# Sigmoid and silu gates written as exponential, logarithm and exponential, with a product on GpSimd

## The chip, the cores and the metric

One core of a Trainium2 chip runs the whole program. The metric is the device time of one execution in microseconds (us). The kernel before took 3142.65 us, the median of 3 runs (3142.52 to 3145.22).

## What is computed

The program is a stack of blocks on 512 tokens of width 1024 in float32. Only its first part matters here: two layers (L = 0, 1) that mix three branches. A convolution branch, a neighbourhood attention over a grid (branch br = 0, 8 heads) and a window attention (br = 1, 8 heads) read one projection of the input. Each is gated, projected, gated again and summed. Layer 0 also carries 256 context tokens, so its tiles have 768 columns; those of layer 1 have 512.

```python
def merge_branches(a_glu, a_gate, o_na, n_gate, o_wa, w_gate, merge, ...):
    y_a = conv_branch(a_glu, a_gate, ...)
    y_b = (o_na * jax.nn.silu(n_gate)) @ w_proj_b
    y_c = (o_wa * jax.nn.silu(w_gate)) @ w_proj_c
    g_a, g_b, g_c = jnp.split(merge, 3, axis=-1)
    y = jax.nn.sigmoid(g_a) * y_a + jax.nn.sigmoid(g_b) * y_b + jax.nn.sigmoid(g_c) * y_c
    return y @ w_o
```

Each of the four silu gates of a layer and branch (units `ag`, 128 channels, two heads each) multiplies the attention's output. The sigmoid gates (`mg` for the attention branches, `cm` for the convolution's; eight of each per layer and branch) multiply the projected outputs.

## The kernel before

TensorE does every product with each float32 operand split in a high and a low part, in three matmuls: 8 steps of 3 matmuls per 512 columns make one chunk of 128 output channels ("lin" steps, line 1795). ScalarE rounds each weight tile (`WH<-RAW`, line 1106) and VectorE takes the rest (`WL<-RAW,WH`, line 1116); for some chunks of the window attention of layer 1 GpSimd does both (lines 1134 and 1125).

`branch` writes the order of the mixing out by hand as a list of units; every engine walks through the same list and takes from it what is its own, so a unit's place in the list is its place in each engine's queue. Attention runs in five phases, one per pair of heads. The scores, exponentials and values of pair p are laid between the projection steps of the chunks for pair p + 1 (`woven`), and a chunk's own after-work is put a number of steps behind its start by `chain`: 8 is right behind its last step. On ScalarE the exponentials of the scores (`Pa<-PS`, `Pb<-PS`, line 1997), the row of maxima (`QB<-PS`, line 2056), the logarithm and exponential of the softmax's denominator (`O<-PS`, `O<-O`, lines 2079 and 2082), the copies of queries and keys (line 2048) and the weight roundings stand in one queue with the gates.

A gate in the woven part is the unit `gev` (silu) or `mgev` (sigmoid) at step 8: one activation from PSUM into one of six tiles T (line 1981). The function tables of silu and of sigmoid are not the one that has exponential and logarithm, so a table load goes before the activation, and behind it the program loads `natural_log_exp_and_others` again (line 1983):

```python
act.activation(buf((nm, "g"))[:, 0:ntk], pairs.of(nm)[:, 0:ntk], ACT.Silu if u[0] == "gev" else ACT.Sigmoid)
if nm not in tail:
    act.preload_act_table_set("natural_log_exp_and_others")
```

The unit `gate`, behind each phase, multiplies the attention's output by the silu gate on GpSimd (`O<-O,T`, line 2286). GpSimd's queue also has copies of queries and keys (line 2270) and the DMAs of the bias tables (BS, line 2291, and BT, line 2296). VectorE lays the taps of the convolution (`C<-AP,SMA,C`, line 1636) between its other work, in the neighbourhood branch alone. The PSUM tiles of the projections are a ring (`pairs`), of which attention borrows two; a gate's PSUM tile is free when its last reader is done. Gates of the tail behind the attention (unit lists `merge` and `proj`) follow one another without a change of table back. `pe_keep` puts a few matmuls of constants in front of certain units (line 1772).

Of the kernel before, what the change touches and what calls it, by code (L numbers as in the profile page):

```python
# [10 lines left out]
ALU = mybir.AluOpType  # L11
# [254 lines left out]
class Plan:  # L266
# [125 lines left out]
    def branch(self, L, br):  # L392
# [11 lines left out]
        def chain(kind, m):  # L404
            nm = (kind, L, br, m)
            if kind == "av":
                return {8: [("vev", nm)], 10: [("vt", nm)], 12: [("vout", nm)]} if br else {8: [("vev", nm)]}
            if kind == "ag":
                return {8: [("gev", nm)]}
            if kind == "mg":  # L410
                return {8: [("mgev", nm)]}
            if kind == "cm":
                return {8: [("mgev", (kind, L, 0, m))], 12: [("paev", ("pa", L, 0, m))]}
            c = {8: [("nrm1", nm)], 11: [("nrm2", nm)], 13 if br else 14: [("nrm3", nm)]}
            if L and br and kind == "aq" and m:
                return {8: [("nrm1", nm)], 12: [("nrm2", nm)], 14: [("nrm3", nm)], 18: [("rot", nm)], 20: [("rot2", nm)]}
            if br:
                c[15] = [("rot", nm)]
                c[16] = [("rot2", nm)]
            return c  # L420
# [68 lines left out]
        for ph in range(5):  # L489
# [26 lines left out]
                    at.setdefault(1 if f else 22 if L and br else 18, []).extend(to)  # L516
            made, late = woven(steps, at, 0, n, heads(ph - 1))
            order += tapped(made, 3 if L == 0 else 5, ph > 0) + ([("gate", L, br, ph - 1, f) for f in range(2)] if ph else [])
        assert not late
        if L == 0 and br:  # L520
            order[4:4] = [("modend", L, 2)]
        order += [("split", ("ag", L, br, m)) for m in range(4)]
# [45 lines left out]
    def attn(self, L, br):  # L568
# [9 lines left out]
        for u in order:  # L578
# [33 lines left out]
            elif kind in ("gev", "mgev"):  # L612
                tmp.take((nm, "g"))
                pairs.release(nm, (nm, "g"))
            elif kind == "pjev":
                pairs.release(nm, ("yp",) + nm[1:] if br else ("y", L, 0, nm[3]))
                tmp.release((("mg",) + nm[1:], "g"), ("y", L, 2 * br, nm[3]))
# [305 lines left out]
def build(nc, t, out):  # L923
# [5 lines left out]
    with ctx:  # L929
# [1011 lines left out]
        def act_attn(act, L, br):  # L1941
            ntk = NTK[L]
# [4 lines left out]
            for u in P.orders[L, br]:  # L1947
# [23 lines left out]
                elif u[0] == "out":  # L1971
                    act_out(act, L, br, nm, u[2])
                elif u[0] == "vev":
                    for dst, src in moved(br, "av", buf((nm, "v")), pairs.of(nm), NT):
                        for w in due("act", ("lin", nm), was((nm, "v"))):
                            act.wait_ge(*w)
                        act.activation(dst, src, ACT.Copy).then_inc(*did("act_v", (nm, "v")))
                elif u[0] in ("gev", "mgev"):
                    for w in due("act", ("lin", nm), was((nm, "g"))):
                        act.wait_ge(*w)  # L1980
                    act.activation(buf((nm, "g"))[:, 0:ntk], pairs.of(nm)[:, 0:ntk], ACT.Silu if u[0] == "gev" else ACT.Sigmoid).then_inc(*did("act_gate", (nm, "g")))  # L1981
                    if nm not in tail:
                        act.preload_act_table_set("natural_log_exp_and_others")
                elif u[0] == "tr":
                    act_rows(act, L, br, u, B)
                elif u[0] == "es":
                    act_sink(act, L, br, u)
                elif u[0] == "fin":
                    act_fin(act, L, br, u)
                elif u[0] == "st":  # L1990
                    p, f, k = u[3:]
                    n = sum(x[2] for x in score_parts(L, br)[k])
                    biased = not br and 2 <= k < 4
                    R = P.pts[L, br]
                    for w in due("act", ("ba" if biased else "sc",) + u[1:], R.after[u], ("masks", L) if br else ("attn", L, br)):
                        act.wait_ge(*w)
                    act.activation(PT[L, br][R.of(u)][:, 0:n], B.of(u)[:, 0:n], ACT.Exp).then_inc(*did("act_ex", ("ex",) + u[1:]))
                elif u[0] == "split":
                    m = nm[3]
                    if m == 0:  # L2000
                        here("act", ("attnout", L, br))
                    for dst, src in gated(L, br, AGH[L, br][:, m, :], OO[L, br][:, m, :]):
                        for w in due("act", ("gated", L, br, m, 0), ("gated", L, br, m, 1), ("attnout", L, br)):
                            act.wait_ge(*w)
                        act.activation(dst, src, ACT.Copy).then_inc(*did("act_g", (nm, "hi")))
# [235 lines left out]
        def pool_attn(pool, L, br):  # L2241
# [11 lines left out]
            for u in P.orders[L, br]:  # L2253
# [4 lines left out]
                elif u[0] == "out" and not (L and br):  # L2258
# [7 lines left out]
                    for dst, at, key in to:  # L2266
                        for w in due("pool", (nm, "y2") if br else (nm, "y"), scores_read(L, br, p - 1, f), ("turn", done["turn"])):
                            pool.wait_ge(*w)
                        done["turn"] += 1
                        pool.tensor_copy(dst, y[at:at + 64, 0:n]).then_inc(*did("pool_st", (nm, key), (nm, "out", f), ("turn", done["turn"])))  # L2270
                elif u[0] == "max" and not br and u[5] == 3 and (u[3], u[4]) != (3, 1):
                    pool_bias_by_query(pool, L, 2 * u[3] + u[4] + 1, [("mx", L, br, u[3], u[4], j) for j in range(4)])
                elif u[0] == "st" and not br and u[5] == 3 and (u[3], u[4]) != (3, 1):
# [1215 lines left out]
```

## Time and profile before

| | us |
|---|---|
| median of 3 runs | 3142.65 |
| the profiled execution, its own time | 3145.4 |
| its span | 3143.6 |
| TensorE matmuls busy | 3029.9 |
| VectorE busy | 1858.6 |
| ScalarE busy | 1282.9 |
| GpSimd busy | 263.7 |
| ScalarE table loads, lines 1981 and 1983 | 50.0 and 41.1 |

The profiled execution took 1.8 us more than its span, and 2.75 us more than the median. Times in the trace are counted from the span's start. The attention phases lie at 190 to 400 us (layer 0, neighbourhood), 650 to 906 (layer 0, window), 1110 to 1340 (layer 1, neighbourhood) and 1440 to 1680 (layer 1, window). Busy shares are averages over stages with different limits; an engine's waits are listed with what released it.

### The profile page before, as it was taken

How to read it: one execution, taken by the hardware profiler on the slowest of the kernel's cores; microseconds unless marked ns; L12 is line 12 of the kernel's file. 1: busy time of each engine (PE TensorE's matmuls, PEld its weight loads, DVE VectorE, ACT ScalarE, POOL GpSimd, SP SyncE). 2: the span in 40 equal slices, each digit the busy share in tenths (PEclk: the TensorE clock that was granted, in tenths of full speed). 3: DMA queues.
4: the chain of work that ended last, by engine and by line, in shares of the span. 5: the costliest groups of instructions: out<-in, count | busy, mean ns of one | idle time of the engine just before them, and what ended most of it. 6: DMA issues, size and time to landing. Idle time of an engine off the chain costs nothing.

```text
span 3143.6 us, 36963 instructions
## 1 busy us (share of the span) xinstructions
PE 3029.9 (96%) x14782; PEld 2393.2 (76%) x14782; DVE 1858.6 (59%) x2959; ACT 1282.9 (41%) x1989; POOL 263.7 (8%) x206
## 2 busy tenths in 40 slices
PE   8999999999999998999999999999999989999998
PEld 5878877877788676767777777788888866788887
DVE  5877675255435667685443787666435675566632
ACT  3244523135532344534554475322225656422222
POOL 0011100001100001102110031000003210000000
PEclk9999999999999999999999999999999989999999
DMA  5222132320012322222112233232332310233332
GB/s 207 72 69 74 48 101 96 109 86 28 21 34 78 104 81 81 67 81 69 47 54 67 83 99 93 94 94 94 96 96 88 121 38 1 81 94 94 94 94 74
DMA packets 78731, 251.49 MB, mean 80 GB/s; under 512 B 9121, under 2 KB 11169, under 8 KB 78561
## 3 DMA queue, kind: packets, MB, share of 16 engines
q1 hardware_dynamic: 72672, 227.91, 22.9%
q0 software_dynamic: 5024, 18.09, 1.8%
q8 instruction: 117, 1.92, 0.3%
q10 hardware_dynamic: 864, 3.15, 0.3%
q14 instruction: 54, 0.43, 0.0%
HBM read 247.01 MB, written 2.10 MB: 79 GB/s over the span
## 4 chain that ended last, share of the span: by engine, by line
PE 45%; ACT 4%; DVE 3%; issue 1%; DMA 0%; POOL 0%; DVEq 0%; ACTq 0%
PE PS L1157 31%; PE PS L1795 4%; PE PS L2815 3%; PE PS L2910 1%; PE PS L1919 1%; ACT WH L1106 1%; PE PS L2875 0%; PE PS L2891 0%; PE PS L2837 0%; ACT PS L2958 0%; PE PS L2876 0%; PE PS L2892 0%; ACT PTN L2972 0%; ACT L1981 0%; PE PS L2543 0%
## 5 line engine op out<-in xcount | busy, mean ns | idle before, releaser
L1116 DVE TENSOR_TENSOR WL<-RAW,WH 128x1024 fp32r<-128x1024 f32 (+3 forms) x374 | 423.7, 1134 | 527.5 <-ACT WH L1106 526.9
L1106 ACT ACTIVATE WH<-RAW 128x1024 fp32r<-128x1024 f32 (+3 forms) x397 | 384.6, 972 | 435.3 <-PE PS L1157 331.0
L1795 PE MATMUL PS<-Hh,WH 128*128 128x512 f32 x1376 | 525.0, 382 | 14.5 <-DVE WL L1116 7.9
L1795 PE MATMUL PS<-Hl,WH 128*128 128x512 f32 x1376 | 487.4, 354 | 0.0
L1795 PE MATMUL PS<-Hh,WL 128*128 128x512 f32 x1376 | 486.1, 353 | 0.0
L1795 PEld LDWEIGHTS PS<-Hh,WH 128*128 128x128 f32 x1376 | 260.0, 189 | 74.6 <-issue 22.7
L1157 PE MATMUL PS<-XH,WH 128*128 128x512 f32 x768 | 305.1, 397 | 0.0
L1157 PE MATMUL PS<-XH,WL 128*128 128x512 f32 x768 | 303.5, 395 | 0.0
L1157 PE MATMUL PS<-XL,WH 128*128 128x512 f32 x768 | 303.5, 395 | 0.0
L1795 PEld LDWEIGHTS PS<-Hl,WH 128*128 128x128 f32 x1376 | 260.3, 189 | 47.6 <-issue 10.1
L1795 PEld LDWEIGHTS PS<-Hh,WL 128*128 128x128 f32 x1376 | 260.3, 189 | 40.3
L1636 DVE SCALAR_TENSOR_TENSOR C<-AP,SMA,C 128x512 f32<-128x512 f32 x360 | 227.0, 692 | 0.5
L1157 PEld LDWEIGHTS PS<-XL,WH 128*128 128x128 f32 x768 | 144.0, 188 | 36.0 <-issue 1.0
L1157 PEld LDWEIGHTS PS<-XH,WH 128*128 128x128 f32 x768 | 144.0, 188 | 35.9 <-issue 1.0
L1157 PEld LDWEIGHTS PS<-XH,WL 128*128 128x128 f32 x768 | 144.0, 187 | 35.2
L1157 PE MATMUL PS<-FGh,WH 128*128 128x512 f32 x384 | 152.2, 396 | 0.0
L1157 PE MATMUL PS<-FGh,WL 128*128 128x512 f32 x384 | 151.8, 395 | 0.0
L1157 PE MATMUL PS<-FGl,WH 128*128 128x512 f32 x384 | 151.7, 395 | 0.0
L1157 PE MATMUL PS<-Hh,WH 128*128 128x512 f32 (+1 forms) x384 | 138.8, 362 | 2.0 <-DVE Hl L1243 1.9
L1157 PE MATMUL PS<-Hl,WH 128*128 128x512 f32 (+1 forms) x384 | 137.1, 357 | 0.0
L1157 PE MATMUL PS<-Hh,WL 128*128 128x512 f32 (+1 forms) x384 | 137.1, 357 | 0.0
L2472 ACT ACTIVATE U<-U 128x512 f32<-128x512 f32 x48 | 30.4, 633 | 253.1 <-DVE U L2503 253.1
(401 smaller groups left out, 5742.1 us busy)
## 6 DMA issues: line engine op xcount, KB each, us to landing
RAW<-in_w_in SPq DMA_DIRECT2D x124, 512.0 KB, 3.6
RAW<-in_ffn_in SPq DMA_DIRECT2D x96, 512.0 KB, 3.6
RAW<-in_ffn_out SPq DMA_DIRECT2D x48, 512.0 KB, 3.5
RAW<-in_w_ada SPq DMA_DIRECT2D x32, 384.0 KB, 3.7
RAW<-in_nsa_in SPq DMA_DIRECT2D x21, 512.0 KB, 3.3
RAW<-in_lru_in SPq DMA_DIRECT2D x20, 512.0 KB, 3.6
MW<-in_w_ada SPq DMA_DIRECT2D x32, 256.0 KB, 9.7
BS<-in_bs POOLq DMA_DIRECT2D x16, 512.0 KB, 3.9
```

Source lines behind the costliest of these rows:

```text
L1106: act.activation(WH[half[j]][:, 0:n], RAW[j % NRAW][:, 0:n], ACT.Copy).then_inc(*did("act_whi", ("whi", j)))
L1116: dve.tensor_tensor(WL[half[j]][:, 0:n], RAW[j % NRAW][:, 0:n], WH[half[j]][:, 0:n].bitcast(F32), ALU.subtract).then_inc(*did("dve_wlo", ( ...
L1157: mm = pe.matmul(ps[:, c:c + n], wt[:, 128 * i:128 * i + 128], x[:, a:a + n], start=(seen == 0 and q == 0), stop=(seen == total - 1 and q ...
L1636: dve.scalar_tensor_tensor(dst, src, wt, dst, ALU.mult, ALU.add).then_inc(*did("dve_tap", ("tap", L, m, k, a0), ("tap", L, m, k)))
L1795: mm = pe.matmul(ps[:, c:c + w_], wt[:, 128 * k:128 * k + 128], x[:, a:a + w_], start=(k == 0 and q == 0), stop=(k == n - 1 and q == 2))
L1919: mm = pe.matmul(dst, VV[L, br][:, b, 64 * g:64 * g + 128], src, start=first, stop=end)
L2472: act.activation(u, u, ACT.Gelu_apprx_tanh).then_inc(*did("act_ge", (a, "gelu")))
L2815: mm = pe.matmul(ps[:, 0:S], wt[half[j]][:, 128 * k:128 * k + 128], x[:, k, :], start=(k == 0 and q == 0), stop=(k == 7 and q == 2))
L2910: mm = pe.matmul(o[64 * f:64 * f + 64, 0:256].rearrange("p (m q) -> p m q", m=2), VN[b][:, kt, g, :], pt[:, f, :, :], start=(b == 0 and kt ...
```

## The change

The woven gates become chains of small steps that need the exponential and logarithm alone: sigmoid(x) = exp(-ln(1 + exp(-x))). `gx1` and `sx1` take exp(-x) from PSUM; `gx1` also copies x out of PSUM into a second tile. `gx2` is ln(1 + e), `gx3` the last exponential. `gx4` multiplies by x on GpSimd, for silu alone. The gates of the tail stay as they were. What is left of the after-work when the last phase ends is now appended to the list, ahead of `split`; before, nothing was.

```diff
             if kind == "ag":
-                return {8: [("gev", nm)]}
+                return {8: [("gx1", nm)], 10: [("gx2", nm)], 11: [("gx3", nm)], 12: [("gx4", nm)]}
             if kind == "mg":
-                return {8: [("mgev", nm)]}
+                return {8: [("sx1", nm)], 10: [("gx2", nm)], 11: [("gx3", nm)]}
             if kind == "cm":
-                return {8: [("mgev", (kind, L, 0, m))], 12: [("paev", ("pa", L, 0, m))]}
+                nm = (kind, L, 0, m)
+                return {8: [("sx1", nm)], 9: [("gx2", nm)], 10: [("gx3", nm)], 12: [("paev", ("pa", L, 0, m))]}
...
-        assert not late
+        for k in sorted(late):
+            order += late[k]
...
+            elif kind == "gx1":
+                tmp.take((nm, "x"))
+                tmp.take((nm, "g"))
+                pairs.release(nm, (nm, "x"), (nm, "e"))
+            elif kind == "sx1":
+                tmp.take((nm, "g"))
+                pairs.release(nm, (nm, "e"))
+            elif kind == "gx4":
+                tmp.release((nm, "x"), (nm, "g"))
...
+                elif u[0] in ("gx1", "sx1"):
+                    if u[0] == "gx1":
+                        for w in due("act", ("lin", nm), was((nm, "x"))):
+                            act.wait_ge(*w)
+                        act.activation(buf((nm, "x"))[:, 0:ntk], pairs.of(nm)[:, 0:ntk], ACT.Copy).then_inc(*did("act_gate", (nm, "x")))
+                    for w in due("act", ("lin", nm), was((nm, "g"))):
+                        act.wait_ge(*w)
+                    act.activation(buf((nm, "g"))[:, 0:ntk], pairs.of(nm)[:, 0:ntk], ACT.Exp, scale=-1.0).then_inc(*did("act_gate", (nm, "e")))
+                elif u[0] == "gx2":
...
+                    act.activation(g, g, ACT.Ln, bias=ones[:, 0:1]).then_inc(*did("act_gate", (nm, "l")))
+                elif u[0] == "gx3":
...
+                    act.activation(g, g, ACT.Exp, scale=-1.0).then_inc(*did("act_gate", (nm, "s" if nm[0] == "ag" else "g")))
...
+                elif u[0] == "gx4":
+                    g = buf((nm, "g"))[:, 0:ntk]
+                    for w in due("pool", (nm, "s"), (nm, "x"), ("turn", done["turn"])):
+                        pool.wait_ge(*w)
+                    done["turn"] += 1
+                    pool.tensor_tensor(g, g, buf((nm, "x"))[:, 0:ntk], ALU.mult).then_inc(*did("pool_g", (nm, "g"), ("turn", done["turn"])))
```

It touches 33 gates: 16 silu (8 per layer) and 17 sigmoid (7 in layer 0, 10 in layer 1). Counted over ScalarE's whole program, 67 of 109 table loads go and 82 activations come; GpSimd gets 16 products. The queues of TensorE, VectorE and SyncE keep their rows and their order.

ScalarE in the window attention of layer 1, at a sigmoid gate (`cm`); in the rows `T<-PS` is the gate, QB the row of maxima and WH a weight rounding. Before:

```order
739 L2079 ACTIVATE O<-PS 64x512
740 L2082 ACTIVATE O<-O 64x512
741 L2048 ACTIVATE QA<-T 64x512
742 L2048 ACTIVATE QB<-T 64x512
743 L1981 ACT_TABLE_LOAD
744 L1981 ACTIVATE T<-PS 128x512
745 L1983 ACT_TABLE_LOAD
746 L2056 ACTIVATE QB<-PS 1x512
747 L1106 ACTIVATE WH<-RAW 128x512
748 L1997 ACTIVATE Pb<-PS 128x512
```

Now (the lines of the changed file are 11 to 35 further down):

```order
754 L2077 ACTIVATE QA<-T 64x512
755 L2077 ACTIVATE QB<-T 64x512
756 L1996 ACTIVATE T<-PS 128x512
757 L2085 ACTIVATE QB<-PS 1x512
758 L1117 ACTIVATE WH<-RAW 128x512
759 L2001 ACTIVATE T<-T,CO 128x512
760 L2006 ACTIVATE T<-T 128x512
761 L2026 ACTIVATE Pb<-PS 128x512
```

Both loads are gone: only the gate's one activation is left between the copies and the row of maxima. The logarithm and the last exponential come behind the weight rounding.

ScalarE in the neighbourhood attention of layer 0, at the second silu gate. Before:

```order
116 L2056 ACTIVATE QB<-PS 1x512
117 L1981 ACT_TABLE_LOAD
118 L1981 ACTIVATE T<-PS 128x768
119 L1983 ACT_TABLE_LOAD
120 L2056 ACTIVATE QB<-PS 1x256
121 L1106 ACTIVATE WH<-RAW 128x1024
122 L2048 ACTIVATE KA<-T 64x768 x2
123 L2048 ACTIVATE QA<-T 64x768
124 L1997 ACTIVATE Pb<-PS 128x512
125 L1997 ACTIVATE Pa<-PS 128x512
```

Now:

```order
118 L1993 ACTIVATE T<-PS 128x768
119 L1996 ACTIVATE T<-PS 128x768
120 L2085 ACTIVATE QB<-PS 1x256
121 L1117 ACTIVATE WH<-RAW 128x1024
122 L2001 ACTIVATE T<-T,CO 128x768
123 L2077 ACTIVATE KA<-T 64x768 x2
124 L2077 ACTIVATE QA<-T 64x768
125 L2026 ACTIVATE Pb<-PS 128x512
126 L2006 ACTIVATE T<-T 128x768
127 L2026 ACTIVATE Pa<-PS 128x512
```

Two activations from PSUM stand for the one with its loads, one more is ahead of the exponentials of the scores, and one between them.

GpSimd at the same place (T is the gate, BT and BS the bias tables). Before:

```order
29 L2270 CAST QB<-T 64x768
30 L2296 DMA BT<-in_bt 128x1024
31 L2291 DMA BS<-in_bs 128x1024
32 L2286 TENSOR_TENSOR O<-O,T 64x512
33 L2286 TENSOR_TENSOR O<-O,T 64x256
```

Now:

```order
30 L2299 CAST QB<-T 64x768
31 L2305 TENSOR_TENSOR T<-T 128x768
32 L2331 DMA BT<-in_bt 128x1024
33 L2326 DMA BS<-in_bs 128x1024
34 L2321 TENSOR_TENSOR O<-O,T 64x512
```

The new product stands between a copy and the issue of the next bias table.

## Rows read from the trace of the kernel before

**Rows 1.** The page: span, and busy time of each engine.
```profile
span 3143.6 us, 36963 instructions
PE 3029.9 (96%) x14782; PEld 2393.2 (76%) x14782; DVE 1858.6 (59%) x2959; ACT 1282.9 (41%) x1989; POOL 263.7 (8%) x206
```

**Rows 2.** Busy time by stretch: PE, PEld, DVE, ACT, POOL, then PEclk, DMA share, GB/s.
```profile
190.00:400.00 210.00, 200.51 (x1102) 167.00 (x1103) 150.66 (x235) 107.87 (x155) 38.04 (x38) 1.00 0.20 63
650.00:906.00 256.00, 243.47 (x1302) 197.05 (x1301) 120.26 (x175) 124.60 (x181) 23.36 (x17) 1.00 0.09 29
1110.00:1340.00 230.00, 210.33 (x1019) 163.51 (x1017) 158.10 (x269) 113.10 (x174) 32.59 (x34) 1.00 0.23 71
1440.00:1680.00 240.00, 226.94 (x1037) 173.49 (x1036) 112.34 (x176) 123.01 (x181) 39.84 (x24) 0.99 0.16 50
```

**Rows 3.** TensorE's waits, 190 to 1700 us: us in total, times, longest.
```profile
PE PS L1899 <- ACT QB L2056: 5.9, 6, 1.8
...
PE PS L1866 <- DVE STAT L2212: 5.8, 5, 2.1
PE PS L1919 <- ACT Pa L1997: 5.5, 7, 1.3
...
PE PS L1919 <- ACT Pb L1997: 4.6, 6, 1.0
...
PE PS L1899 <- ACT Pa L1997: 2.1, 2, 1.2
...
PE PS L1795 <- DVE Gl L2139: 1.4, 2, 0.7
...
PE PS L1841 <- ACT T L1981: 1.2, 2, 0.6
```

**Rows 4.** ScalarE's groups by shape, 190 to 1700 us: busy us, mean ns.
```profile
L1981 ACT ACT_TABLE_LOAD x39 | 50.0, 1283 | 11.3 <-PE PS L1795 10.8
L1983 ACT ACT_TABLE_LOAD x32 | 41.1, 1283 | 0.6
...
L1981 ACT ACTIVATE T<-PS 128x768 f32<-128x768 f32 x32 | 26.0, 812 | 108.2 <-PE PS L1795 108.0
```

**Rows 5.** ScalarE in order of time at one sigmoid gate: start us, us.
```profile
1506.92 1.28 ACT L1981 ACT_TABLE_LOAD   x1 [0.56 <-PE PS L1795]
1508.22 0.60 ACT L1981 ACTIVATE T<-PS 128x512 f32<-128x512 f32 x1
1508.83 1.28 ACT L1983 ACT_TABLE_LOAD   x1
1510.13 0.58 ACT L2056 ACTIVATE QB<-PS 1x512 fp32r<-1x512 f32 x1
```

**Rows 6.** TensorE in order of time, at three of its waits.
```profile
262.35 1.12 PE L1919 MATMUL PS<-Pb,V 128*128 128x512 f32 x2 [0.72 <-ACT Pb L1997]
...
1510.76 0.50 PE L1899 MATMUL PS<-QA,KA 128*128 128x512 f32 x1 [1.41 <-ACT QB L2056]
...
1655.97 0.59 PE L1899 MATMUL PS<-QA,KA 128*128 128x512 f32 x1 [1.76 <-ACT QB L2056]
```

**Rows 7.** Busy time by stretch, around the third of them.
```profile
1656.00:1659.00 3.00, 3.00 (x8) 2.33 (x9) 0.56 (x1) 1.70 (x3) 0.00 (x0) 0.54 0.29 87
```

**Rows 8.** VectorE and GpSimd in order of time, layer 0, neighbourhood.
```profile
263.59 1.15 DVE L1636 SCALAR_TENSOR_TENSOR C<-AP,SMA,C 128x512 f32<-128x512 f32 x2
...
265.05 0.70 DVE L2129 TENSOR_TENSOR PS<-PS,BT 128x512 f32<-128x512 f32 x1 [0.31 <-PE PS L1900]
...
338.19 3.37 DVE L1636 SCALAR_TENSOR_TENSOR C<-AP,SMA,C 128x512 f32<-128x512 f32 x2
...
338.56 2.71 POOL L2286 TENSOR_TENSOR O<-O,T 64x512 f32<-64x512 f32 x2
```

**Rows 9.** GpSimd products: mean ns by shape, and one alone in time.
```profile
L2286 POOL TENSOR_TENSOR O<-O,T 64x768 f32<-64x768 f32 x8 | 14.6, 1830 | 98.8 <-DVE O L2239 93.1 <-ACT T L1981 5.5 <-POOL QB L2270 0.2
...
1653.16 1.28 POOL L2286 TENSOR_TENSOR O<-O,T 64x512 f32<-64x512 f32 x1 [19.49 <-DVE O L2239]
```

More of the change, by code:

```diff
@@ L1977, in act_attn @@
                         act.activation(dst, src, ACT.Copy).then_inc(*did("act_v", (nm, "v")))
+                elif u[0] in ("gx1", "sx1"):
[8 more added lines that the diff above has]
+                    g = buf((nm, "g"))[:, 0:ntk]
+                    for w in due("act", (nm, "e"), ("co",)):
+                        act.wait_ge(*w)
+                    act.activation(g, g, ACT.Ln, bias=ones[:, 0:1]).then_inc(*did("act_gate", (nm, "l")))
+                elif u[0] == "gx3":
+                    g = buf((nm, "g"))[:, 0:ntk]
+                    for w in due("act", (nm, "l")):
+                        act.wait_ge(*w)
+                    act.activation(g, g, ACT.Exp, scale=-1.0).then_inc(*did("act_gate", (nm, "s" if nm[0] == "ag" else "g")))
                 elif u[0] in ("gev", "mgev"):
@@ L2270, in pool_attn @@
                         pool.tensor_copy(dst, y[at:at + 64, 0:n]).then_inc(*did("pool_st", (nm, key), (nm, "out", f), ("turn", done["turn"])))
+                elif u[0] == "gx4":
+                    g = buf((nm, "g"))[:, 0:ntk]
+                    for w in due("pool", (nm, "s"), (nm, "x"), ("turn", done["turn"])):
+                        pool.wait_ge(*w)
+                    done["turn"] += 1
+                    pool.tensor_tensor(g, g, buf((nm, "x"))[:, 0:ntk], ALU.mult).then_inc(*did("pool_g", (nm, "g"), ("turn", done["turn"])))
                 elif u[0] == "max" and not br and u[5] == 3 and (u[3], u[4]) != (3, 1):
```

## The prediction

> **What bounds the kernel now.** The page first: TensorE's matmuls are busy for 3029.9 of 3143.6 us, ScalarE for 1282.9 [rows 1]. So TensorE is the bound, and a change on ScalarE can only give back what TensorE waits for it. Its own instructions don't change: its queue keeps every row. Next the four attention stretches, where all touched gates lie [rows 2]: 936 us, of which TensorE is busy for 881.3. The 54.8 us left are all that any change of waits could give there. Third, who ended those waits [rows 3]. The five ScalarE rows make 19.3 us (one more, for a PSUM tile that a gate held, has 0.6). The rest is for VectorE, mainly norm and maximum chains that begin with TensorE's own results, so they move with it.
>
> Fourth, what a gate costs ScalarE's queue. A load takes 1.28 us, an activation of 768 columns 0.81 [rows 4], one of 512 columns 0.60 [rows 5]. The instructions behind a load start within 0.02 us of its end: at 1506.92 the load, at 1508.22 the gate, at 1508.83 the load back, at 1510.13 the row of maxima that TensorE has been waiting for, 1.41 us [rows 5, 6]. A gate thus holds the queue for 3.37 us in layer 0 (1.28 + 0.81 + 1.28) and 3.16 in layer 1, and the loads are three quarters of it.
>
> **ScalarE, by place in its queue.** Busy time: 67 loads go, 67 x 1.283 = 86.0 us. 82 activations come: in layer 0 three for each of 8 silus and two for each of 7 sigmoids, 38 at 0.81; in layer 1 8 x 3 + 10 x 2 = 44 at 0.60; together 57.2 us. Net 28.8 us less, to about 1254. What counts is how early the next instruction starts. In layer 0, behind a silu gate's first step (copy and exponential), the queue is 3.37 - 1.62 = 1.75 us ahead of before; behind the logarithm 0.94; behind the last exponential 0.13. Behind a sigmoid gate 2.56, 1.75 and 0.94. In layer 1 the silu gives 1.96, 1.36 and 0.76, the sigmoid 2.56, 1.96 and 1.36. None is negative: by work queued, nothing on ScalarE comes later than before. A PSUM tile is free sooner too: 1.62 us after a silu gate begins where it was 2.09.
>
> The trace in order of time has 22 waits of TensorE for ScalarE, of 0.3 to 1.8 us, within 8 us of a gate's second load: 8 in layer 0 (6.2 us), 5 in layer 1's neighbourhood attention (3.4), 9 in its window attention (8.5); three of them stand in rows 6. I took each against the lead at its place in the new order. The wait of 0.72 us at 262.35 [rows 6] is for Pb, behind the logarithm of a silu: the lead of 0.94 takes it away. The 1.41 at 1510.76 has a lead of 2.56. The 1.76 at 1655.97 is for a row of maxima behind a weight rounding and a logarithm, lead 1.36: 0.4 stays. Of the pair 0.89 and 0.80 around 1635 to 1638, 1.36 of 1.69 goes; one of 0.35 in layer 0 keeps 0.22. Sum: 6.0 + 3.4 + 7.7 = **17.1 us**.
>
> Two chains through ScalarE end on VectorE. One wait of 1.28 us for a maximum, one of the five in rows 3, is for a VectorE queue that had stood still for a weight rounding behind a gate: 1.2 us. The two for Gl at the attention's ends, 1.4 us [rows 3], follow from softmax denominators that stood behind a load: 1.3 us. The late logarithms and exponentials of the last gates, which now stand ahead of the split, lie beside VectorE's and GpSimd's work on the same heads; uncovered they would cost 2 x 0.81. That makes 19.6 us.
>
> **GpSimd and VectorE.** 16 products come: 8 of 768 columns at 1.83 us and 8 of 512 at 1.28 [rows 9], 24.9 us, if the time goes by columns. GpSimd is busy for 263.7 us [rows 1], but its new product can hold others. A pair of convolution taps takes 1.15 us alone and 3.37 beside a GpSimd product; that product, a 512 and a 256 part, took 2.71 too [rows 8]. So the two engines don't run two-operand work from SBUF side by side. The neighbourhood attention has taps and VectorE busy for 69 to 72% of the time; the window attention has no taps and 47% [rows 2]. The first layer 0 products come some 0.3 us after the first of these taps at 263.59. The bias addition at 265.05 [rows 8] is right behind them, and an exponential and TensorE's next values hang on it. A product in front can push it by up to 1.8 us. Bounds: nothing, if each product falls into an idle stretch or if the two share without loss; 24.9 us, if all 16 stand in TensorE's way in full. The row nearest is that of the taps, which only the 8 neighbourhood products meet: I take 0.4 us each, **3 us**, well towards the lower end, since TensorE's waits for maxima at present, 5 in 190 to 1700 us, are 5.8 us in all though GpSimd's two-operand parts already run there (24 in the two neighbourhood stretches). The bias table's DMA issue now stands behind the product. GpSimd is busy for only 38.0 of 210 us there [rows 2], so that idle queue covers it; without that cover it would be 1.83 us late.
>
> The Trainium skill has this as a rule ("SBUF — State Buffer", summary for kernel authors): a VectorE operation with two SBUF inputs and a GpSimd one that reads SBUF exclude each other, the second waits for the first to finish. The taps agree with it. By that rule each meeting costs the length of the other operation, which is the upper end above.
>
> **What the lead is worth.** A wait taken away makes TensorE come sooner to the next one. Chains that start from its own results follow; those that are paced by VectorE's queue do not, above all in layer 1's neighbourhood attention (VectorE 69%, TensorE idle for 19.7 of 230 us [rows 2]). Bounds: nothing lost, or half of 19.6. I take 3 us.
>
> Sum: 19.6 - 3 - 3 = **13.6 us**. The profiled execution's 3145.4 us becomes 3131.8. The median of the runs is 2.75 below the profiled execution; from 3142.65 the forecast is **3129.0 us**.
>
> On the table loads the skill speaks otherwise than the rows. "ScalarE: Activation LUTs" (section on what a table load costs) puts a switch at about 2.66 us, a load of 1.28 and a drain of 1.38. Rows 5 show no drain: gate and load follow within 0.02 us. By the page 67 switches would be 178 us of ScalarE's time, an estimate; the waits of TensorE are measured and their sum would hardly change.
>
> **Rivals.**
>
> *All of it, and the clock.* TensorE's clock is at the upper of its two levels (2.4 GHz, granted 1.00) nearly throughout; after the wait of 1.76 us it was granted 0.54 for 3 us [rows 7], mostly the lower level, 1.2 GHz. Such a spell costs 3 x 0.46 = 1.4 us. If the wait is cut to 0.4 and the spell goes with it, and neither VectorE's queue nor the products take anything, the gain is 19.6 + 1.4 = 21.0 us: 3121.6. For it: the leads are two to four times as long as most waits. Against it: VectorE's load in the neighbourhood stretches. 0.17.
>
> *The waits move instead.* The row of maxima or the exponential that TensorE waited for arrives sooner, but its next need then waits for VectorE, and the last exponential of the gate stands in front of a score's exponential where the lead is only 0.13. Price: half the gain of the window stretches (4.4 us in layer 0 and 7.7 in layer 1) and none of the neighbourhood's, less 3 for the products: 3.0 us, 3139.6, which is within 0.2%. For it: 35 of the 54.8 us of idle time aren't ScalarE's. 0.17.
>
> *The products stop VectorE where TensorE waits for it.* Slower by this one mechanism: each product makes taps, weight remainders (`WL`) or the copies' remainders wait for its full length, and the PSUM bank of a maximum comes free that much later. All 16 in full are 24.9 us against 19.6: slower by 5.3, 3148. With the excess of the taps in rows 8 (3.37 - 1.15 = 2.2 us for a product's two parts) 16 meetings would be 35 us and 3158. It decides from 1.2 us of exposed waiting per product. Against it: only half of the products meet taps, and in the window stretches VectorE is idle for half of the time. 0.05.
>
> *The change doesn't do what it says.* A load could stay where a step needs another table. The new order has no load between the woven steps, so this has 0.01, with the time of before.
>
> **Numbers.** Forecast 0.60, from 3124 to 3136. A measurement of this kernel can tell about 0.2%, 6.3 us: faster means below 3136.4. Faster: 0.60 and 0.17, and 0.03 of the moved waits, 0.80. Within 0.2%: the rest of the moved waits and some of the products, 0.16. Slower: 0.04. The range goes from 3121 to 3140: it takes in the whole gain and most of the moved waits, and leaves out the slower case.
>
> **What would show it.** 42 table loads on ScalarE in all, and its busy time near 1254 us; GpSimd near 289; TensorE's busy time within 3 us of before. TensorE's waits for QB, Pa and Pb from 18.1 us (the first four ScalarE rows of rows 3) to under 4; the ones at 1510.76 and 262.35 gone, that at 1655.97 at 0.4 or less. Waits for the maxima (L2212) would grow by up to 3 us. It is wrong if the waits for ScalarE go and the time doesn't follow; if they stay, though the loads are gone; or if taps beside the new products make the bias additions late by more than 1 us each.

## The result, and the profile after

The changed kernel took 3119.1 us, the median of 5 runs (3116.5 to 3122.3), against 3143.75 for the kernel before in the same comparison (5 runs, 3142.5 to 3149.5). The ratio is 0.9919, with a 95% interval of 0.9905 to 0.9932: 24.6 us faster. The forecast was 13.6 us, and the result lies 2 us below the lower end of the range. A second comparison, on another chip (with the experiments, below), gave 3121.2 against 3144.1, ratio 0.9924 [0.9911, 0.9936], 22.9 us; its median would lie just inside that end.

The page of the changed kernel, span and busy time of each engine, against [rows 1]:

```profile
span 3120.5 us, 37010 instructions
PE 3027.4 (97%) x14782; PEld 2395.6 (77%) x14782; DVE 1868.7 (60%) x2959; ACT 1252.7 (40%) x2004; POOL 304.7 (10%) x222
```

ScalarE is at 1252.7 us where 1254 were forecast, and TensorE's busy time is 2.5 us less. GpSimd has 41.0 us more, where 24.9 had been counted for the products. The stretches between (names of columns as in [rows 2]) say where the time went:

```profile
190.00:400.00 210.00, 201.37 (x1111) 168.36 (x1111) 157.80 (x238) 106.04 (x162) 54.18 (x42) 1.00 0.21 63
650.00:906.00 256.00, 249.16 (x1341) 203.13 (x1341) 126.77 (x181) 125.43 (x190) 30.76 (x21) 1.00 0.10 31
1110.00:1340.00 230.00, 213.49 (x1029) 166.90 (x1028) 166.44 (x272) 108.97 (x181) 42.88 (x38) 0.99 0.23 73
1440.00:1680.00 240.00, 235.35 (x1075) 182.08 (x1074) 116.45 (x177) 111.23 (x187) 40.31 (x24) 0.99 0.16 50
```

These are stretches of time and hold somewhat later work than before. In both window stretches TensorE is idle for much less, 6.8 and 4.7 us for 12.5 and 13.1. In the first neighbourhood stretch it is idle for 8.6 us, and was for 9.5: there little came. That can be read to the microsecond, since TensorE's queue has the same matmuls in the same order: set beside each other by their number, the changed kernel is 0.2 us behind at 645 us, 6.9 ahead at 906, 12.2 at 1340 and 22.4 at 1680. The stretch from 1735 to the end adds 0.7: a low-clock spell there was longer before.

TensorE's waits, 190 to 1700 us of the changed kernel, against [rows 3]:

```profile
PE PS L1806 <- DVE WL L1127: 9.9, 9, 2.9
PE PS L1859 <- ACT T L2049: 5.9, 5, 1.9
...
PE PS L1877 <- DVE STAT L2241: 4.5, 4, 2.1
...
PE PS L1930 <- ACT Pb L2026: 3.5, 3, 1.4
...
PE PS L1910 <- ACT Pa L2026: 0.9, 1, 0.9
PE PS L1930 <- ACT Pa L2026: 0.8, 1, 0.8
...
PE PS L1910 <- ACT Pb L2026: 0.4, 1, 0.4
```

No wait for QB is left (5.9 us before) and none for a gate's PSUM tile. Waits for Pa and Pb fell from 12.2 to 5.6 us, of which 2.5 are new (below), and those for maxima from 5.8 to 4.5. What stays on top is behind VectorE's weight remainders (10.1 us before) and behind T L2049, the inverse roots of the queries' and keys' norms (5.9 before too): the gates hardly touch these.

ScalarE's groups by shape, same stretch, against [rows 4]:

```profile
L2001 ACT ACTIVATE T<-T,CO 128x768 f32<-128x768 f32 x15 | 14.0, 930 | 0.2
...
L2001 ACT ACTIVATE T<-T,CO 128x512 f32<-128x512 f32 x18 | 12.9, 715 | 0.1
L2006 ACT ACTIVATE T<-T 128x768 f32<-128x768 f32 x15 | 12.6, 839 | 0.2
```

The logarithm takes 0.93 us for 768 columns and 0.72 for 512, 0.12 more than the 0.81 and 0.60 of the prediction, and the last exponential 0.84. So the smallest lead of the prediction, 0.13 us behind a silu gate of layer 0, was in truth none (3.37 - 1.62 - 0.93 - 0.84 = -0.02).

Now one place, the sigmoid gate of [rows 5]. TensorE in order of time before, the matmul ahead of the wait and the second one behind it (between them stands the one of 1510.76, [rows 6]):

```profile
1508.96 0.40 PE L1795 MATMUL PS<-CGh,WL 128*128 128x512 f32 x1
...
1511.10 0.39 PE L1900 MATMUL PS<-QB,KB 65*128 65x512 f32 x1
```

The same three in the changed kernel:

```profile
1496.48 0.39 PE L1806 MATMUL PS<-CGh,WL 128*128 128x512 f32 x1
1496.71 0.40 PE L1910 MATMUL PS<-QA,KA 128*128 128x512 f32 x1
1496.94 0.39 PE L1911 MATMUL PS<-QB,KB 65*128 65x512 f32 x1
```

The idle time shown was 1.41 us. From start to start it was 1.80 before and is 0.23 now, 1.57 less; then 0.34 before and 0.23 now, 0.11 less. Together the gate gave back 1.68 us, 0.27 more than the idle time. The difference has two parts that the rows show: a matmul of 0.40 us lies over its successor's start by 0.17 when nothing waits, and the first one behind a wait starts its successor 0.11 late. (The profile models the ends of matmuls, so idle time between them is a modelled figure; the starts are not.)

A gate can also cost TensorE time where the view shows no idle time at all. Before, at a silu gate of layer 0:

```profile
257.99 0.27 PE L1795 MATMUL PS<-Hh,WL 128*128 128x256 f32 x1
258.31 0.50 PE L1899 MATMUL PS<-QA,KA 128*128 128x512 f32 x1
```

and in the changed kernel:

```profile
258.04 0.28 PE L1806 MATMUL PS<-Hh,WL 128*128 128x256 f32 x1
258.16 0.40 PE L1910 MATMUL PS<-QA,KA 128*128 128x512 f32 x1
```

From start to start 0.32 us became 0.12. The view lists no wait, since the matmul before it covers all but 0.04 us.

Last, ScalarE's order in the changed kernel at the sigmoid gate above:

```profile
1494.37 0.60 ACT L1996 ACTIVATE T<-PS 128x512 f32<-128x512 f32 x1 [0.49 <-PE PS L1806]
1494.99 0.59 ACT L2085 ACTIVATE QB<-PS 1x512 fp32r<-1x512 f32 x1
1495.61 0.63 ACT L1117 ACTIVATE WH<-RAW 128x512 fp32r<-128x512 f32 x1
```

The row of maxima is done at 1495.58, 1.1 us before TensorE comes for it.

### The profile page after: what moved, and what is told of

Read it like the earlier page. It is cut to its first block, busy times and chain, and to the rows that moved or that the text cites. A ratio compares the mean times of both kernels' runs of the same rounds, so it can differ in the third digit from the quotient of the medians.

```text
span 3120.5 us, 37010 instructions
## 1 busy us (share of the span) xinstructions
PE 3027.4 (97%) x14782; PEld 2395.6 (77%) x14782; DVE 1868.7 (60%) x2959; ACT 1252.7 (40%) x2004; POOL 304.7 (10%) x222
## 3 DMA queue, kind: packets, MB, share of 16 engines
q1 hardware_dynamic: 72672, 227.91, 22.9%
## 4 chain that ended last, share of the span: by engine, by line
PE 47%; ACT 3%; DVE 3%; issue 1%; DMA 0%; DVEq 0%; ACTq 0%
PE PS L1168 32%; PE PS L1806 5%; PE PS L2850 3%; PE PS L2945 1%; PE PS L1930 1%; PE PS L2910 0%; ACT WH L1117 0%; PE PS L2926 0%; PE PS L2872 0%; ACT PS L2993 0%; PE PS L2911 0%; PE PS L2927 0%; ACT PTN L3007 0%; PE PS L2578 0%; PE PS L1910 0%
## 5 line engine op out<-in xcount | busy, mean ns | idle before, releaser
L1806 PEld LDWEIGHTS PS<-Hh,WH 128*128 128x128 f32 x1376 | 260.5, 189 | 74.3 <-issue 21.6
L1806 PEld LDWEIGHTS PS<-Hl,WH 128*128 128x128 f32 x1376 | 260.9, 190 | 48.3 <-issue 10.1
L1136 POOL TENSOR_TENSOR WL<-RAW,WH 128x1024 fp32r<-128x1024 f32 (+1 forms) x33 | 78.8, 2389 | 572.3 <-ACT WH L1117 571.5
```

Of the source, the lines that this page charges most:

```text
L1136: pool.tensor_tensor(WL[half[j]][:, 0:n], RAW[j % NRAW][:, 0:n], WH[half[j]][:, 0:n].bitcast(F32), ALU.subtract).then_inc(*did("pool_wlo", ...
L1806: mm = pe.matmul(ps[:, c:c + w_], wt[:, 128 * k:128 * k + 128], x[:, a:a + w_], start=(k == 0 and q == 0), stop=(k == n - 1 and q == 2))
```

## The experiments

**An account of the time.** The traces are compared on one stretch that is cut by matmuls, not by time: from TensorE's matmul that started at 190.17 before to the one at 1735.17. It holds all four attention stretches. In it I take three sums: the idle time shown for TensorE's waits (those of over 0.15 us, which the view lists), their number, and the time in which the granted clock was 0.5, that is at the lower of the two levels, 1.2 GHz. Such a spell is charged with half of its length. The theory that the first comparison gave: *gain = waits less, by the idle time shown, + 0.27 us for each wait fewer, + half of the low-clock time less.* The 0.27 comes from places of the first trace pair; the other kernels test it.

| kernel | waits, us (number) | low clock, us | gain by the account | gain measured |
|---|---|---|---|---|
| before | 71.4 (78) | 10.2 | | |
| changed | 52.3 (52) | 17.1 | 22.7 | 22.6 |
| changed, again | 51.8 (52) | 10.2 | 26.6 | 26.2 |
| exponential alone | 49.4 (51) | 20.5 | 24.2 | 25.2 |
| no product | 50.6 (50) | 13.7 | 26.6 | 26.3 |
| product on VectorE | 51.7 (52) | 20.5 | 21.6 | 21.6 |
| window gates only | 57.6 (62) | 17.1 | 14.7 | 14.1 |
| neighbourhood gates only | 66.8 (68) | 10.2 | 7.3 | 8.3 |
| loads back | 106.0 (85) | 47.8 | -55.2 | -54.5 |
| product later | 49.6 (50) | 13.7 | 27.7 | 27.5 |
| product later, again | 49.7 (50) | 20.5 | 24.2 | 24.6 |
| steps spread | 52.1 (52) | 13.7 | 24.6 | 25.5 |
| one more copy | 59.2 (67) | 20.5 | 10.1 | 11.1 |

It holds within about 1 us for each. A fit of both factors to the twelve rows gives 0.27 us for a wait and 0.48 for the low-clock time. The idle time alone would give 19.1 for the changed kernel.

The 0.27 is a mean, not the price of each wait. Matmul by matmul, 28 waits went between before and changed. At 17 of them the start of the second matmul came 0.24 to 0.27 us sooner than the idle time accounts for, at the other eleven -0.05 to 0.22; together 5.3 us. Another 1.9 us came at seven places like 258.31, where no wait was listed (five for QB, two for Gl). That is 7.2 us, or 0.26 for each listed wait.

The two traces of the changed kernel are one program, and differ by 3.6 us, nearly all of it through low-clock time (6.9 us, half is 3.4). So a median can hide 3 us. Where it matters I compare at like clock: a line through the 59 runs of these kernels, with one slope (1.9 us for 0.001 of mean granted clock) and a level for each kernel, leaves 1.3 us of scatter a run. The levels at 0.993 are 3120.7 for the changed kernel, 3117.4 exponential alone, 3118.0 no product, 3121.1 product on VectorE, 3117.6 product later, 3120.5 spread, 3133.1 one more copy; each is known to 0.4 to 0.7 us. Half of the low-clock time would make the slope 3.1; the clocks on record are rounded to 0.001, which may flatten it, and with 3.1 these levels move by under 1 us. With the 37 runs of the kernel before that stand beside these, it has the level 3146.8, 26.1 above the changed kernel; the account without its clock term gives 19.1 + 26 x 0.27 = 26.1.

**Exponential alone.** The kernel before, its 32 woven gates that had a load back reduced to one exponential without loads; the gate's function is left out.

```diff
-act.activation(buf((nm, "g"))[:, 0:ntk], pairs.of(nm)[:, 0:ntk], ACT.Silu if u[0] == "gev" else ACT.Sigmoid).then_inc(...)
 if nm not in tail:
-    act.preload_act_table_set("natural_log_exp_and_others")
+    act.activation(buf((nm, "g"))[:, 0:ntk], pairs.of(nm)[:, 0:ntk], ACT.Exp, scale=-0.001).then_inc(...)
+else:
+    act.activation(buf((nm, "g"))[:, 0:ntk], pairs.of(nm)[:, 0:ntk], ACT.Sigmoid).then_inc(...)
```

> The kernel before, with a single exponential in place of each of 32 woven silus and sigmoids and no table load beside it; what the gate computes is left out, so neither the logarithm, the second exponential, the copy of x nor the product on GpSimd is there. Theory A (loads only, and each wait of TensorE costs about 0.27 us more than the profile shows as idle, because the matmul before it is overlapped in steady state and the matmul behind it starts slower): all waits behind gates go and nothing comes in their place, a gain of 29 to 31 us over the kernel before, near 3113 us. Theory B (the 13.6 us of the prediction were right for the loads and the change's other gain comes from the new steps, for instance PSUM tiles that come free sooner): a gain of about 20 us, near 3124 us.

Measured: 3119.1 us, ratio 0.9913 [0.9899, 0.9926], between the two numbers by the median. Its runs had a mean granted clock of 0.9926, those of the kernel before in the same comparison 0.9937. At like clock it is 29.4 us below the kernel before, and its account without the clock term is 22.0 + 27 x 0.27 = 29.3: that is the first theory. ScalarE is busy for 1201.9 us, 50.8 less than in the changed kernel, for the same time in the median. Against the kernel without products the level is 0.6 us lower, within the noise. So 51 us of activations on ScalarE cost almost nothing, and lead beyond what the changed kernel has is worth almost nothing.

**No product.** The changed kernel without what `gx4` does: silu gates stay sigmoids, so that factor of the result is left out. The last exponential now tells the readers that the gate is done:

```diff
-act.activation(g, g, ACT.Exp, scale=-1.0).then_inc(*did("act_gate", (nm, "s" if nm[0] == "ag" else "g")))
+act.activation(g, g, ACT.Exp, scale=-1.0).then_inc(*did("act_gate", (nm, "g")))
...
-elif u[0] == "gx4":
...
-    pool.tensor_tensor(g, g, buf((nm, "x"))[:, 0:ntk], ALU.mult).then_inc(*did("pool_g", (nm, "g"), ("turn", done["turn"])))
```

> The changed kernel without the product of silu on GpSimd (silu gates are left as sigmoids; the copy of x stays). Theory A (the product blocks VectorE's two-operand work in the neighbourhood attention and so costs time): 4 to 5 us faster than the changed kernel, near 3114.5 us, with no wait of TensorE for Pb at 262 to 268 us and near 1280 us. Theory B (the product is covered everywhere, and what the neighbourhood stretches lose comes from the added activations): within 1 us of the changed kernel's 3119.

Measured: 3118.9 us, ratio 0.9916 [0.9902, 0.993]. By the median the second theory; but in its trace the waits for Pb are fewer:

```profile
PE PS L1930 <- ACT Pb L2026: 1.0, 1, 1.0
```

That is 2.5 us and two waits less. Its runs had a mean granted clock of 0.9925, those of the changed kernel 0.9936. This left the product's price open.

**Product later.** The layer 0 and 1 products of the neighbourhood branch four steps on:

```diff
-return {8: [("gx1", nm)], 10: [("gx2", nm)], 11: [("gx3", nm)], 12: [("gx4", nm)]}
+return {8: [("gx1", nm)], 10: [("gx2", nm)], 11: [("gx3", nm)], 16 if not br else 12: [("gx4", nm)]}
```

> The changed kernel with the product of silu four steps later in the neighbourhood attentions (16 in place of 12). Theory A (in layer 0's neighbourhood attention two products, at 267 and 329 us, hold up the tap that stands ahead of a bias addition; 1.40 and 1.14 us of waits for Pb and 0.27 us more each): both waits go, 2 to 3 us faster, near 3116.5 us. Theory B (the product meets other two-operand work wherever it is put there): the waits move to other matmuls and the time stays at 3119.

Measured: 3118.8 us, ratio 0.9914 [0.9901, 0.9928]. The medians again say nothing, but the traces show the mechanism. The changed kernel, VectorE, GpSimd, ScalarE and TensorE in order of time at the first of the two products that cost something:

```profile
262.03 1.47 DVE L2230 TENSOR_TENSOR QA<-T,QA 64x768 fp32r<-64x768 f32 x1
...
262.84 2.34 POOL L2305 TENSOR_TENSOR T<-T 128x768 f32<-128x768 f32 x1
...
263.53 2.60 DVE L1647 SCALAR_TENSOR_TENSOR C<-AP,SMA,C 128x512 f32<-128x512 f32 x2
266.16 1.30 DVE L2158 TENSOR_TENSOR PS<-PS,BT 128x512 f32<-128x512 f32 x2
...
266.89 0.60 ACT L2026 ACTIVATE Pb<-PS 128x512 f32<-128x512 f32 x1 [4.65 <-DVE PS L2158]
...
267.55 1.13 PE L1930 MATMUL PS<-Pb,V 128*128 128x256 f32 x4 [1.40 <-ACT Pb L2026]
```

The same place with the product later:

```profile
264.82 1.15 DVE L1647 SCALAR_TENSOR_TENSOR C<-AP,SMA,C 128x512 f32<-128x512 f32 x2
266.00 0.70 DVE L2158 TENSOR_TENSOR PS<-PS,BT 128x512 f32<-128x512 f32 x1
...
267.38 1.13 PE L1930 MATMUL PS<-Pb,V 128*128 128x256 f32 x4
...
269.02 1.86 POOL L2305 TENSOR_TENSOR T<-T 128x768 f32<-128x768 f32 x1
```

The pair of taps takes 1.15 us without a product beside it and 2.60 with one; the product takes 1.86 in its later place and 2.34 here. Its record begins while VectorE's operation before the taps, also with two inputs in SBUF, still runs (262.03 to 263.50). The bias addition follows 1.45 us late, behind it the exponential, and TensorE waits 1.40 us. A second place like it is at 329.07, with 1.14 us; the other 14 products open no wait. The exclusion rule of the Trainium skill ("SBUF — State Buffer", summary for kernel authors) fits this row to 0.2 us: the taps would start when the product ends, at 265.18, and end at 266.33; they end at 266.13. By the same rule the product would run from 263.50 to 265.36, and it ends at 265.18, though its record starts at 262.84.

**Both again, beside each other.** The changed kernel and the one with the product later, unchanged, on one chip.

> The changed kernel once more, as it is, on the chip of the next run. What is open: in the traces the kernel with the layer 0 product four steps later (product_late) and the one without products have both waits for Pb beside the first products gone (some 3 us with what hangs on each), but their medians lay within 1 us of the changed kernel's, in different calls and at other mean granted clocks (0.9928 and 0.9925 over their runs, 0.9936 for the changed kernel's). Theory A (the product costs what the trace shows, the low-clock spells of the runs hid it): beside each other, and with the times set against the mean granted clock of each run (0.001 of it is about 3 us: half of the time at the lower level), the changed kernel is 3 to 4 us longer than product_late. Theory B (it costs nothing that lasts): within 1 us at like clock. Its median 3117 to 3122 either way.

> The kernel with the layer 0 product four steps later once more, beside the changed one. Theory A: at like granted clock 3 to 4 us less than the changed kernel, median 3114 to 3119. Theory B: within 1 us of it at like clock.

Measured: 3121.2 us, ratio 0.9924 [0.9911, 0.9936], and 3118.5, ratio 0.991 [0.9896, 0.9923]. Run by run at like clock: at 0.995 it is 3116.5 and 3113.9, at 0.992 3124.2 and 3122.9 against 3120.8 and 3118.5. Over all four sets of runs the levels differ by 3.1 us, known to 0.6. The first theory: the products cost some 3 us, in two places, and the later product gives them back. It is the shortest of the kernels here that compute the whole result.

**Product on VectorE.** `gx4` in VectorE's queue at the same place:

```diff
-pool.tensor_tensor(g, g, buf((nm, "x"))[:, 0:ntk], ALU.mult).then_inc(...)
+dve.tensor_tensor(g, g, buf((nm, "x"))[:, 0:ntk], ALU.mult).then_inc(...)
```

> The changed kernel with the product of silu on VectorE at the same place in the order. Theory A (what costs is VectorE blocked for GpSimd's full 1.3 to 1.8 us or more): VectorE itself needs about 0.7 to 0.95 us, so half of the loss comes back, 2 us faster than the changed kernel, near 3117 us. Theory B (VectorE's queue is what paces the neighbourhood stretches): any work put on it costs its own length there, 8 x 0.8 us, and the time is 3 us or more above the changed kernel, 3122.

Measured: 3122.4 us, ratio 0.9928 [0.9915, 0.994], the number of the second theory; but its runs had the lowest clock of these kernels (0.9922 on average), and at like clock it is 0.4 us from the changed kernel, which can't be told from nothing. A product takes 0.95 us on VectorE for 768 columns and 0.69 for 512. In the trace the three waits for Pb are shorter than the changed kernel's 3.5 us, but none is gone:

```profile
PE PS L1930 <- ACT Pb L2026: 2.3, 3, 1.0
```

The two behind the products are 0.82 and 0.55 us for 1.40 and 1.14, and one for the norms' roots at 289.48 is 1.03 for 0.40. So on VectorE the product delays what stands behind it less, and half of that is lost at another place; on the whole no difference between the engines is shown.

**Window gates only, neighbourhood gates only.** In the one, the neighbourhood branch keeps the gates of before, in the other the window branch (`if br` for `if not br`).

```diff
+if not br and kind in ("ag", "mg", "cm"):
+    return {8: [("gev" if kind == "ag" else "mgev", nm)]} if kind != "cm" else {8: [("mgev", (kind, L, 0, m))], 12: [("paev", ("pa", L, 0, m))]}
```

> New gates in the two window attentions alone; the neighbourhood attentions keep silu and sigmoid with their table loads. Theory A (the gain is a sum of local waits): the two traces put side by side give 6.9 us in layer 0's window attention and 9.8 in layer 1's, so 16.7 us faster than the kernel before, 3127 us. Theory B (part of the gain of a stretch is only there because the stretch before ended sooner): under 13 us.

> New gates in the two neighbourhood attentions alone. Theory A (local waits, additive, products costing 4 to 5 us there): 1.5 us in layer 0 and 5.4 us in layer 1, 6 to 8 us faster than the kernel before, near 3137 us; together with the kernel that changes the window attentions alone it makes the whole change's 24.6 us. Theory B (not additive): the two sums differ from 24.6 by more than 4 us.

Measured: 3128.2 us (ratio 0.9947 [0.9935, 0.996]) and 3137.6 (ratio 0.997 [0.9959, 0.9982]), 15.9 and 9.2 us less than the kernel before in their comparisons (3144.1 and 3146.9). The second is a little more than the 6 to 8 expected. Together 25.1 against the changed kernel's 24.6, and in the cut stretch of the traces 14.1 + 8.3 = 22.4 against 22.6: the parts add up, and none feeds on the other.

**Loads back.** The changed kernel with two loads at each of the 33 gates, 66 in all: one at the gate's head, once its projection is done, and one in front of the first exponential. Between them stands only silu's copy of x. In the kernel before, one stood ahead of the activation and one behind it, so the gate's PSUM tile comes free later here.

```diff
+for w in due("act", ("lin", nm)):
+    act.wait_ge(*w)
+act.preload_act_table_set("sigmoid_and_others")
 if u[0] == "gx1":
...
+act.preload_act_table_set("natural_log_exp_and_others")
 act.activation(buf((nm, "g"))[:, 0:ntk], pairs.of(nm)[:, 0:ntk], ACT.Exp, scale=-1.0)
```

> The changed kernel with both table loads put back at each of the 33 gates, ahead of the first activation and ahead of the first exponential; the new steps stay. Theory A (only the loads were in the way): every lead is gone and the added activations put ScalarE 0.6 to 2.4 us behind the kernel before at each gate, so it is slower than the kernel before, by 5 to 15 us, 3149 to 3159 us, and TensorE's waits for QB, Pa and Pb are above 18 us. Theory B (the spread over steps or the sooner release of PSUM gave the gain): it stays 5 us or more below the kernel before.

Measured: 3196.2 us, ratio 1.0154 [1.014, 1.0168]: 49 us longer than the kernel before beside it and 77 longer than the changed kernel of the first comparison, and 37 beyond the upper end of what was expected. Of the two theories the first one has the sign. ScalarE's busy time grew by 85.9 us, 1.30 for each load. ScalarE in order of time at the gate of 1494.37 above:

```profile
1553.81 1.28 ACT L1992 ACT_TABLE_LOAD   x1 [0.48 <-PE PS L1806]
1555.10 1.28 ACT L1999 ACT_TABLE_LOAD   x1
```

and TensorE's waits, 190 to 1700 us:

```profile
PE PS L1910 <- ACT QB L2089: 14.0, 12, 2.3
PE PS L1930 <- ACT Pa L2030: 10.2, 7, 2.5
...
PE PS L1930 <- ACT Pb L2030: 6.4, 6, 1.6
...
PE PS L1859 <- ACT T L2000: 5.0, 2, 2.6
PE PS L1852 <- ACT T L2000: 5.0, 2, 2.5
```

The places of [rows 3] are back, longer, and the gate's own PSUM tile (T L2000) adds 10 us. The expectation had no clock in it: 47.8 us at the lower level where before had 10.2, 18.8 us of the time. One of the spells, busy time by stretch:

```profile
357.00:360.00 3.00, 2.69 (x10) 2.40 (x11) 1.59 (x2) 2.95 (x5) 1.11 (x2) 0.51 0.03 5
```

**One more copy.** The changed kernel with one activation from PSUM more ahead of each gate's exponential, 22 us on ScalarE.

```diff
+act.activation(buf((nm, "g"))[:, 0:ntk], pairs.of(nm)[:, 0:ntk], ACT.Copy).then_inc(*did("act_gate", (nm, "e0")))
+for w in due("act", (nm, "e0")):
+    act.wait_ge(*w)
 act.activation(buf((nm, "g"))[:, 0:ntk], pairs.of(nm)[:, 0:ntk], ACT.Exp, scale=-1.0)
```

> The changed kernel with one more activation (a copy from PSUM) at each of the 33 gates, ahead of the first exponential: 0.81 us each in layer 0 and 0.60 in layer 1, 22 us of ScalarE. Theory A (before the change ScalarE stood exactly where TensorE began to wait, and the lead of 0.1 to 2.6 us at each gate is only partly used): most of it falls into the lead, TensorE waits 2 to 6 us more, near 3123 us. Theory B (each microsecond put behind a gate costs TensorE one, as putting the loads back did): 22 us or more, above 3138 us.

Measured: 3132.0 us, ratio 0.9958 [0.9945, 0.997], 12.9 longer than the changed kernel, between the numbers. Waits for ScalarE are back at some places and not at others:

```profile
PE PS L1930 <- ACT Pb L2029: 3.3, 5, 1.0
PE PS L1930 <- ACT Pa L2029: 2.5, 3, 0.9
PE PS L1910 <- ACT QB L2088: 1.9, 3, 0.8
```

Fifteen small waits come beside those of the changed kernel: eleven for ScalarE, one for a maximum, one for Gl, and two put down to "issue". By the account they cost 15 x 0.27 = 4.1 us beside 6.9 us of idle time shown.

**Steps spread.** Logarithm and last exponential later (steps 12 and 14 of `ag` and `mg`, product at 16; `cm` one step later), so that the exponentials of the scores stand in front of them.

```diff
-return {8: [("gx1", nm)], 10: [("gx2", nm)], 11: [("gx3", nm)], 12: [("gx4", nm)]}
+return {8: [("gx1", nm)], 12: [("gx2", nm)], 14: [("gx3", nm)], 16: [("gx4", nm)]}
...
-return {8: [("sx1", nm)], 10: [("gx2", nm)], 11: [("gx3", nm)]}
+return {8: [("sx1", nm)], 12: [("gx2", nm)], 14: [("gx3", nm)]}
...
```

> The changed kernel with the small steps further apart: silu at 8, 12, 14 and 16, sigmoids of the attention branches at 8, 12 and 14, those of the convolution branch at 8, 10 and 11. Theory A (small steps right behind the gate still use up lead that scores need): the wait of 0.8 us at 1638 us of the kernel before and the two for Pb in layer 0 go, 3 to 4 us faster, near 3115.5 us. Theory B (where ScalarE is ahead, the place of a step is worth nothing): as the kernel with the product alone moved.

Measured: 3119.1 us, ratio 0.9918 [0.9905, 0.9932], and 2.9 us above the later product at like clock: neither theory. The two Pb waits are gone as with the later product, the one of 0.8 us at 1638 of the kernel before is not, and new ones came:

```profile
PE PS L1877 <- DVE QA L2230: 2.9, 2, 1.5
```

Queries that VectorE finishes late, two waits. What in VectorE's queue pushed them was not tried apart.

## Why the size was wrong and the sign right

**What bounds the kernel, and the leads: right.** The 28.8 us of waits for ScalarE in the cut stretch are 14.1 now. The waits at 262.35 and 1510.76 are gone and the one at 1655.97 shows no idle time. No place that the leads cleared kept a wait but one: that of 1638.47 is still 0.80 us long. ScalarE's busy time (1252.7 for 1254) and the fall of the maxima (5.8 to 4.5) came as worked out. The waits for QB, Pa and Pb are 5.6 us, where under 4 had been said: 2.5 of them are the products' own.

**The step that failed is the price of a wait**, the term 19.6. The prediction took each of the 22 waits, 17.1 us, and the two chains of 2.5 at the idle time that the profile shows. In shown idle time the trace fell by 19.1 net. The products had opened two waits of 2.5 us together, so 21.7 and 28 waits had gone, 2.1 more than the 19.6: among them two of 0.55 us that the profile put down to "issue" (783.40 and 840.84), and some that were to keep a rest. To this come 28 x 0.27 = 7.6 us that no row of idle time shows (7.2 by the starts of the matmuls, of which 1.9 at places where no wait was listed at all). That is 29.3 us where the prediction had 19.6.

**The term for a lost lead failed too, with 3 us.** I had set it against a TensorE that comes sooner to its next wait. Next to nothing was lost: in the stretches, beside the two waits of the products, one for VectorE grew (from 1.28 to 1.57 us, at 255.9) and one shrank (from 1.02 to 0.58, at 1454.1), the two branches add up, and the account closes without such a term.

**The products: right in size, by luck in part.** 3 us forecast, 3.1 by shown idle time and 0.27 each, and 3.1 by like clock. But not 0.4 at each of eight: two of them cost all of it. A product took 2.07 us on average for 768 columns (1.81 to 2.65) and 1.51 for 512 (1.26 to 1.77), not 1.83 and 1.28. Copies on GpSimd (`QB<-T`) went from 1.13 to 1.62 us and from 0.89 to 1.40; without products they are as long (1.57 and 1.40), so the products are not the reason. That mostly idle engine hid both.

**The clock: missing in the sum, and no gain as the rival had it.** The rival's spell at 1656 did go, but others came, at 485 and 1281 us, and the one at 1465 (1479 before) lasts twice as long: 17.1 us in the profiled run for 10.2, that is 3.4 us back. In the other trace of the same program it was 10.2 as before, so this term is of the run as much as of the change.

By steps in the cut stretch: 29.3 - 3.1 - 3.4 = 22.8, measured 22.6; the profiled executions as a whole differ by 23.1 (3145.4 to 3122.3) and the medians by 24.6. Of the 9.2 us between 13.6 and 22.8, the waits make 9.7, the lost lead 3, the products -0.1 and the clock -3.4. The range was too narrow because every case in it, the rival with all of the gain too, counted waits at their shown idle time.

**Why 51 us more on ScalarE cost almost nothing, and 86 cost 77.** Three rates, at ScalarE's work added: from the exponential alone to all steps (without products) 51 us for 0.6; one more copy 22 us for 12.4 at like clock; two loads a gate 86 us for 77. The first lies within the lead, most of it behind the row of maxima (16 copies of x, 11 us, are ahead of it); the second takes the lead up at about half of the places; the third has none left, and the clock and the PSUM tile join. The copies and loads stand at the gate's head and the logarithms behind, so place and amount are not told apart by these runs.

## What to carry to other kernels

Where one engine is the bound and waits in small pieces, count the waits as well as their idle time: here each was worth 0.27 us on average beyond what is shown, so that 28 waits of 0.8 us were worth a third more. A function-table switch was worth taking out of the queue here even for three activations in its place, with the steps behind the first put behind what the bound engine needs next. Two medians with 3 us between them say little when the mean granted clock of the runs differs by 0.001 or 0.002: compare at like clock, or read the traces by matmul number.

## What the hardware showed that was not expected

The same wait, in two runs of one program, is followed by a low-clock spell in one and not in the other. The changed kernel, behind a wait of 2.08 us for the taps:

```profile
484.92 2.40 PE L1675 MATMUL PS<-T,CO 128*128 128x512 f32 x4 [2.08 <-DVE T L1705]
...
487.54 0.63 PE L1806 MATMUL PS<-Hl,WH 128*128 128x512 f32 x1
487.97 0.63 PE L1806 MATMUL PS<-Hh,WL 128*128 128x512 f32 x1
```

The changed kernel again, behind the same wait, here 1.75 us:

```profile
484.74 1.56 PE L1675 MATMUL PS<-T,CO 128*128 128x512 f32 x4 [1.75 <-DVE T L1705]
...
486.38 0.40 PE L1806 MATMUL PS<-Hl,WH 128*128 128x512 f32 x1
486.61 0.40 PE L1806 MATMUL PS<-Hh,WL 128*128 128x512 f32 x1
```

Matmuls of 512 columns follow one another after 0.43 us in the first and 0.23 in the second. Busy time by stretch, 486 to 489, first the changed kernel:

```profile
486.00:489.00 3.00, 3.00 (x9) 2.22 (x7) 1.65 (x3) 0.65 (x1) 0.00 (x0) 0.51 0.00 0
```

and again:

```profile
486.00:489.00 3.00, 3.00 (x21) 2.12 (x20) 2.66 (x4) 1.65 (x2) 0.00 (x0) 1.00 0.06 11
```

The granted clock is 0.51 and 1.00. Matmul by matmul the spell costs 1.6 us, nearly as much as the wait itself. All thirteen traces have this wait. Six have a spell behind it, with waits of 1.91 to 2.21 us, and seven have none, with waits of 1.73 to 2.04. The longer waits have it more often, but the two groups overlap, so the length alone doesn't decide. What else does stays open; no run here was made for it.
